# Arena tiles moved to a 128-byte boundary and split-weight slots set 8208 bytes apart

## What is computed

```
def swiglu_ffn(h, w_gu, w_down):
    gate, up = jnp.split(h @ w_gu, 2, axis=-1)
    return (jax.nn.silu(gate) * up) @ w_down
...
        p = h @ w_in
...
        merged = (jax.nn.sigmoid(gate_a) * (y_a @ w_proj_a[layer])
                  + jax.nn.sigmoid(gate_b) * (y_b @ w_proj_b[layer]))
        x = x + merged @ w_out[layer]
...
        sh1, sc1, g1, sh2, sc2, g2 = jnp.split((silu_c @ ada_w[i] + ada_b[i])[:, None, :], 6, axis=-1)
...
    u = t @ w_up
    ...
    return (jax.nn.silu(g) * a) @ w_down
```

## The kernel before

| tile | start, bytes | past a 128-byte boundary |
|---|---|---|
| `raw` | 16512 | 0 |
| `w_hi`, slot s | 32896 + 8192 s | 0 |
| `w_lo`, slot s | 65664 + 8192 s | 0 |
| `X`, `HA_hi`, `HA_lo`, `K_` | 98432, 106624, 114816, 123008 | 0 |
| small tiles from `SS` to `GT`, with `CB` | 129248 to 132063 | 96 |
| `arena` and each tile in it (`FT_*`, `HB_*`, `XN`, `BC`, `XC`, `WA`, `LORT`, `WST` ...) | 132064 + KB x 1024 | 96 |

## Time and profile before

### The profile page before, as it was taken

The page is one execution under the profiler, slowest core; times in us unless marked ns, Lnnn a source line. Parts: engine busy times, 40 slices in busy tenths (PEclk is TensorE's granted clock), DMA queues, the critical chain, the costliest instruction groups (busy, mean ns, idle before and its releaser), DMA issues.

```text
span 2721.0 us, 45474 instructions
## 1 busy us (share of the span) xinstructions
PE 2608.7 (96%) x18123; PEld 2089.3 (77%) x18123; DVE 1688.3 (62%) x1913; ACT 1391.1 (51%) x1633; POOL 81.0 (3%) x113
## 2 busy tenths in 40 slices
PE   7999989999999999989999999989999999998998
PEld 6887567888888886568878878757888887876886
DVE  5545646855555546657665555687776776455675
ACT  4434434634445434334545444575774764465673
POOL 0002000000000001001000000000000000011000
PEclk9999999999999999999999999999999999989999
DMA  5547743544444459444544544304445444523453
GB/s 209 190 177 237 268 153 124 202 184 180 187 175 185 185 180 326 168 169 160 197 172 185 187 169 174 150 1 156 172 185 193 161 185 173 197 93 106 155 185 124
DMA packets 77707, 474.79 MB, mean 174 GB/s; under 512 B 9358, under 2 KB 13564, under 8 KB 27248
## 3 DMA queue, kind: packets, MB, share of 16 engines
q1 hardware_dynamic: 64656, 437.42, 43.6%
q0 software_dynamic: 8288, 30.93, 3.4%
q10 hardware_dynamic: 4608, 4.20, 0.6%
HBM read 463.81 MB, written 2.13 MB: 171 GB/s over the span
## 4 chain that ended last, share of the span: by engine, by line
PE 78%; DMA 10%; DVE 6%; ACT 3%; issue 1%; DVEq 1%; ACTq 0%; POOL 0%; SPq 0%; POOLq 0%
PE ACC L481 70%; DMA ADW<-wada 5%; DMA raw<-wstream 3%; PE TP L557 3%; PE MM L481 2%; DVE w_lo L1668 2%; ACT w_hi L1147 1%; PE TP L481 1%; PE TP L959 1%; DMA BIAS<-toe 0%; DMA PREV<-V 0%; DVE ST L2205 0%; DMA COL<-cols 0%; DVE PR L2217 0%; ACT XX L1303 0%
## 5 line engine op out<-in xcount | busy, mean ns | idle before, releaser
L1668 DVE TENSOR_TENSOR w_lo<-raw,w_hi 128x2048 fp32r<-128x2048 f32 (+2 forms) x371 | 836.2, 2273 | 369.5 <-ACT w_hi L1147 355.0
L1147 ACT ACTIVATE w_hi<-raw 128x2048 fp32r<-128x2048 f32 (+2 forms) x371 | 699.6, 1904 | 393.2 <-DMA raw<-wstream 306.7
L481 PE MATMUL ACC<-w_hi,HA_hi 128*128 128x512 f32 (+1 forms) x2032 | 800.7, 394 | 12.6 <-DVE w_lo L1668 6.9
L481 PE MATMUL ACC<-w_hi,HA_lo 128*128 128x512 f32 (+1 forms) x2032 | 792.0, 390 | 0.1
L481 PE MATMUL ACC<-w_lo,HA_hi 128*128 128x512 f32 (+1 forms) x2032 | 790.7, 389 | 0.0
L481 PEld LDWEIGHTS ACC<-w_hi,HA_hi 128*128 128x128 f32 x2032 | 383.5, 189 | 92.9 <-issue 12.8
L481 PEld LDWEIGHTS ACC<-w_hi,HA_lo 128*128 128x128 f32 x2032 | 383.1, 189 | 80.5 <-issue 0.3
L481 PEld LDWEIGHTS ACC<-w_lo,HA_hi 128*128 128x128 f32 x2032 | 383.9, 189 | 75.8
L481 PE MATMUL ACC<-w_hi,FT_hi 128*128 128x512 f32 x616 | 246.1, 399 | 0.0
L481 PE MATMUL ACC<-w_hi,FT_lo 128*128 128x512 f32 x616 | 244.2, 396 | 0.0
L481 PE MATMUL ACC<-w_lo,FT_hi 128*128 128x512 f32 x616 | 244.1, 396 | 0.0
(11 more groups left out here) (340 smaller groups left out, 2832.0 us busy)
## 6 DMA issues: line engine op xcount, KB each, us to landing
raw<-wstream SPq DMA_DIRECT2D x367, 1024.0 KB, 4.8
ADW<-wada SPq DMA_DIRECT2D x56, 512.0 KB, 3.7
ADW<-wada SPq DMA_DIRECT2D x20, 1024.0 KB, 14.8
BC<-vecs POOLq DMA_DIRECT2D x14, 512.0 KB, 5.9
BIAS<-toe ACTq DMA_DIRECT2D x32, 128.0 KB, 2.8
BC<-mod_scr POOLq DMA_DIRECT2D x6, 512.0 KB, 5.0
MU<-mus POOLq DMA_DIRECT2D x2, 1280.0 KB, 11.3
WA<-lora POOLq DMA_DIRECT2D x2, 1024.0 KB, 10.4
```

Of the source, the lines that this page charges most:

```text
L481: return pe.matmul(*a, skip_group_check=True, **k)
L1147: act.activation(w_hi[:, s, 0:w], unit[:, 0:w], ACT.Copy).then_inc(sem["hi_ready"], 1)
L1668: dve.tensor_tensor(w_lo[:, s, 0:w], unit[:, 0:w], w_hi[:, s, 0:w].bitcast(F32), ALU.subtract).then_inc(sem["lo_ready"], 1)
```

## The change

```
-        w_hi = sb("w_hi", [P, SPLIT, UNIT], F32R)
-        w_lo = sb("w_lo", [P, SPLIT, UNIT], F32R)
-        ADW = sb("ADW", [P, ADA_SLOTS, UNIT], at=ring)
+        w_hi = sb("w_hi", [P, SPLIT, UNIT + 4], F32R)[:, :, 0:UNIT]
+        w_lo = sb("w_lo", [P, SPLIT, UNIT + 4], F32R)[:, :, 0:UNIT]
+        ADW = sb("ADW", [P, ADA_SLOTS, UNIT + 4], at=ring)[:, :, 0:UNIT]
...
-        arena = place["at"]
+        arena = (place["at"] + 127) // 128 * 128
```

## The result

| | median | lowest to highest | runs |
|---|---|---|---|
| before | 2725.95 us | 2718.1 to 2731.4 | 5 |
| changed | 2740.98 us | 2738.7 to 2746.0 | 5 |

The ratio is 1.0061, with a 95% interval of 1.0044 to 1.0079, so 12 to 22 us slower where 20 us faster was forecast. The range held the time; the sign was wrong. One of the rivals, "it is the distance between the two reads that counts", had given 2742 us.

What follows compares the result with a forecast made beforehand. TensorE's stream matmuls were taken to bound the kernel (busy 96% of the span). Arena -20 us, slots, split and landing 0: 2721.0 - 20 = 2701, carried to the runs' median as 2709 us; range 2680 to 2775.

Steps and rivals of the forecast that it cites:

- it is the distance between the two reads that counts: Rival: stream matmuls cost by distance between stationary and moving tiles; +12 us, 2742 us, chance 0.10.
- What bounds the kernel: Whole span: TensorE holds 78% of the chain, so start-to-start time of stream matmuls counts; one stretch is `ADW`'s load.
- Part one, the arena: Matmuls with `FT` and `HB`: aligning the arena saves 7.4 ns on each of 2808, 20.8 us, taken as 20.
- what is left is where the stationary tile lies: Step in part one: loops and clock excluded, so 96 bytes past the boundary makes the 7.4 ns.
- Part two, the slots: Moving operands `w_hi` and `w_lo` of 8904 stream matmuls, at new 16-byte steps: cost taken as zero.
- The slot price of 7.4 ns on five sixths of the stream: Rival: stream matmuls whose weights start off a 128-byte boundary, some 7420, pay 7.4 ns; 2764 us, chance 0.22.
- The rival that came true: The distance rival: mean 230.6 ns for all stream matmuls, +12 us, 2742 us, chance 0.10.
- Part three and four: ScalarE and VectorE writing `w_hi` and `w_lo` (1918, 2290 ns), and `ADW`'s landing in the slots: both cost nothing.
- The upper bound of +15 us for landings at odd multiples of 16 bytes: `ADW` loads: 14 chain pieces at 1.1 us more each; as the slow landing rival 2724 us, chance 0.05.
- How much reaches the end: Down projections and `HB` blocks: nothing else is late, so 20 of the 20.8 us stream gain arrives.

Runs made afterwards that it cites:

- arena_only: Kernel before with only the arena moved to begin on a 128-byte boundary, slots still 8192 bytes apart; 2717.5 us against 2723.3, ratio 0.998.
- all_32_off: Kernel before with the arena at the weights' place modulo 512 and every tile 32 bytes later, off 64-byte boundaries; 2703.8 us, ratio 0.9935.
- lo_64: Kernel before with `w_hi`, `HA` and arena at one place modulo 512, only `w_lo` 64 bytes further on; 2741.7 us against 2724.5.
- weights_16_off: Kernel before with all weights and `HA` 16 bytes past a 128-byte boundary, `FT` at 0 past, `HB` at 32 past; 2736.1 us against 2728.3.
- arena_at_weights: Kernel before with the arena moved to the weights' place modulo 512, slots still 8192 bytes apart; 2707.7 us against 2723.3, ratio 0.9949.
- slots_only: The change without its arena line: slots 8208 bytes apart, arena still 96 past a 128-byte boundary; 2744.4 us against 2723.3, ratio 1.0084.

## Why the prediction was wrong, point by point

**What bounds the kernel**: right. The time changed as the start-to-start distances of the stream changed, +25 us from them against +23 in the profiled spans and +15 between the medians. What else moves the time is the granted clock, a few us from one execution to the next: the profiled execution of `arena_only` is 3 us longer than that of before (2724.3 against 2721.0 us), though its stream is 5 us shorter.

**Part one, the arena**: the step that failed is "what is left is where the stationary tile lies". The rows had excluded the loops, the clock and the weight load by itself, rightly; but `HA` and `FT` differ in two things that the trace before can't separate, their place past a boundary and their distance from the weights. I took the first, called it the price, and carried it over whole. `all_32_off` shows that it is the second, and `arena_only` that the move to the boundary gives 1.9 of the 7.4 ns (-5.8 us at the end, 0 to 11 by its interval), since its distance went only from 352 to 384. The row that should have warned me was in my own argument: a load that costs nothing alone and something beside a full stream speaks of two readers, hence of both their addresses.

**Part two, the slots**: the value 0 failed, and it was said to be the weakest step. The cost is 5.1 ns on every `HA` matmul. Three things in the change can make it, and each was seen alone: `HA` lost distance 0 (6 to 7.5 ns at most other distances), `w_hi` and `w_lo` of a slot came 64 bytes apart (5 ns in `lo_64`), and half of the slots stand at an odd multiple of 16 (4 ns). They don't add up; each alone already gives 4 to 7.5, and the changed kernel reads 5.1. How they combine isn't shown: in the changed kernel the two slots at odd multiples of 16 (232.5 and 230.5 ns) are no slower than the other two (231.2 and 234.5). The slot price of 7.4 ns on five sixths of the stream, 2764 us, was too high for this reason, and because `FT` and `HB` had nothing left to lose.

The Trainium skill, "TensorE: Matmul & The Clock Gate", section "Step-by-step: what each phase is for", says that the streamed operand and the weight load have read ports of their own and that loading the next tile doesn't take read bandwidth from the running matmul. The runs disagree: with the same stream, 226.8 to 234.3 ns by the place of the tile that is loaded. The prediction took from the note on cachelines in "SBUF — State Buffer" of the Trainium skill, which stands in the section "Door 1: The DMA port swizzle" and not in "Terms", that all addresses which begin a 16-byte line are alike. The note itself speaks of consecutive accesses and not of starts. That reading is contradicted once more by `weights_16_off`, whose weights start at a 16-byte line and cost 4 ns.

**The rival that came true** took the mean of two known distances for the two unknown ones, 230.6 ns and +12 us. Its mechanism is shown in steps of 32 bytes, its time was met (2741), but its picture was too simple: the period is 256 bytes and not 64, there is no halfway value, and unequal distances among the three passes cost by themselves. That its time came out is partly luck: it put `HA` up by 3.7 ns and the others down by 3.7, +12 us in all, where 5.1 up and 2.3 down, +25 us, were measured; part of that did not reach the medians, and it started from 2729.5 us where the five executions of before have a median of 2725.95.

**Part three and four**, the split at 1919 and 2290 ns and the landing of `ADW` at 3.8 us, were right. The upper bound of +15 us for landings at odd multiples of 16 bytes was not needed.

**How much reaches the end.** The forecast took nearly all of a change in the stream to the end. In `arena_at_weights` it is 7.2 ns x 2808 = 20 us in the stream and 14 us (9 to 19) at the end, in `all_32_off` 18 (11 to 24); for the loss 25 in the stream and 17 (12 to 22). So 0.7 to 0.9 of it by the medians. Part of this scatter is the granted clock: the 18 executions of before beside these runs go from 2717.9 us at a mean granted clock of 0.990 to 2732.0 at 0.984. A straight line through the 43 executions of before, `arena_only`, `slots_only`, `arena_at_weights` and `all_32_off`, with a level for each kernel, gives 1.9 to 2.0 us for each 0.001 of the clock. At equal clock, by this estimate, the four stand at -4, +23, -17 and -17 us from before (each within 2 to 4), where the stream changed by -5, +24, -20 and -20. So the arena at the weights' place gains the same 17 us with or without the 32 bytes, and over four fifths of a change reaches the end. Where the rest goes is not shown; stretches that TensorE doesn't set, as that of `ADW`, are a likely place.

**The version that beats both** came out of the same runs: slots 8192 bytes apart and the arena at the place of the weights, 2707.7 us, 0.51% under before (0.33 to 0.68), or with all of it 32 bytes later 2703.8 us. That is the gain of some 20 us that the forecast had, from another rule.

## What to carry to other kernels

Where TensorE streams float32r in matmuls of 512 columns as here, with a weight load for each, put the stationary tiles at the same place modulo 256 bytes as the tiles that stream past them, in all slots and for both halves of a split weight. A skew of the slots cost 2% of each `HA` matmul here. Other types and widths were not tried. When a trace shows two classes of the same instruction, list everything in which their operands differ, distances between them included, before naming one as the cause. And a reason that a part is slow does not price a second part for which no row exists: such a part deserves the range's full width and a look at who already pays nothing.

## What the runs showed of the hardware that was not expected

- A stream matmul of 512 columns takes 226.8 ns when its operands are 0 modulo 256 bytes apart, 228.9 to 230.1 at 192, and 232.3 to 234.3 at the six other multiples of 32.
- If one of three passes in turn has another distance (0, 192, 0), all three take 232 ns (`lo_64`).
- With the weights at an odd multiple of 16 bytes a matmul takes 230.9 ns at distance 0; with the weights on a 32-byte boundary an activation 16 bytes below their place costs next to nothing (227.5), one 16 above takes 231.0.
- Loading 64 stationary columns in place of 128, and writing half the output partitions, made the matmul slower where it had been fastest (227.3 to 230.1).
- Transfers of 512 KB land in 3.80 us in slots at odd multiples of 16 bytes and in 3.78 in the others. With half of the slots at such addresses ScalarE writes `w_hi` in 1919 ns and VectorE `w_lo` in 2290, against 1918 and 2290 before.
